# The first block's output projection in pairs of output tiles: seven half products in place of eight

## The reference, cut to what matters

```python
merged = g_ssm * (y_ssm @ w_proj_ssm) + g_att * (y_att @ w_proj_att)
x = x + gate * (merged @ w_out)        # w_out is 1024 x 1024
return rmsnorm(x, final_norm_w)        # goes into the second block
```

## Time and profile before

| | |
|---|---|
| median of 3 executions | 1833.75 us (1833.32 to 1833.89) |
| the profiled execution | 1833.91 us, its span 1832.4 us |
| PE busy | 1802.9 us (98%) |
| DVE, ACT, POOL busy | 1221.2 (67%), 744.7 (41%), 217.2 (12%) us |
| granted clock of TensorE, mean | 0.996 |
| stage 7, first matmul to first small product | 1111.45 to 1199.04 us |

### The profile page before, as it was taken

One profiled execution on the slowest core, in us unless ns is written; L12 is line 12 of the kernel. 1 busy time (PEld: TensorE's weight loads), 2 busy tenths in 40 slices (PEclk: granted clock), 3 DMA queues, 4 the chain that ended last, 5 costly groups with the idle time before them and its releaser, 6 DMA issues.

```text
span 1832.4 us, 26756 instructions
## 1 busy us (share of the span) xinstructions
PE 1802.9 (98%) x9827; PEld 1481.0 (81%) x9827; DVE 1221.2 (67%) x1630; ACT 744.7 (41%) x1145; POOL 217.2 (12%) x355
## 2 busy tenths in 40 slices
PE   7999999999999999999999999999999999999998
PEld 5788888888888888888888888878777778888886
DVE  4796455475377888888888444469366667676876
ACT  4423545553234454444445342353144445432422
POOL 2000011010102222012220000022100002110100
PEclk8999999999999999999999999999999999999999
DMA  9633765353611212122122843343311112210412
GB/s 298 236 62 64 153 120 104 99 155 120 184 58 47 81 58 61 42 80 80 58 57 103 296 145 99 117 131 95 112 35 49 37 34 58 58 47 22 146 33 104
DMA packets 176751, 180.45 MB, mean 98 GB/s; under 512 B 11171, under 2 KB 151896, under 8 KB 175768
## 3 DMA queue, kind: packets, MB, share of 16 engines
q1 hardware_dynamic: 162728, 129.95, 22.8%
q0 software_dynamic: 13920, 49.37, 11.5%
q10 hardware_dynamic: 16, 0.00, 0.0%
HBM read 138.80 MB, written 40.50 MB: 98 GB/s over the span
## 4 chain that ended last, share of the span: by engine, by line
PE 77%; PEld 12%; issue 3%; DVE 3%; ACT 2%; DMA 1%; DVEq 1%; SPq 0%; PEldq 0%; POOL 0%; POOLq 0%; ACTq 0%
PE acc L296 23%; PE acc L1713 16%; PE acc L315 14%; PEld acc L315 8%; PE acc L1741 3%; PE acc L3310 3%; PE work L1723 3%; PEld acc L296 2%; PE work L1733 2%; PE work L2743 1%; PE acc L621 1%; PE acc L2752 1%; PE work L2732 1%; PE acc L3648 1%; PEld acc L1115 1%
## 5 line engine op out<-in xcount | busy, mean ns | idle before, releaser
L315 PE MATMUL acc<-ha_hi,w_hi 128*128 128x512 f32 x640 | 257.4, 402 | 1.9 <-DVE nxt L2613 1.1
L315 PE MATMUL acc<-ha_hi,w_lo 128*128 128x512 f32 x640 | 249.9, 390 | 0.0
L315 PE MATMUL acc<-ha_lo,w_hi 128*128 128x512 f32 x640 | 249.3, 390 | 0.0
L276 DVE TENSOR_TENSOR w_lo<-w_raw,w_hi 128x1024 fp32r<-128x1024 f32 x94 | 115.4, 1228 | 92.8 <-ACT w_hi L272 90.5
L272 ACT ACTIVATE w_hi<-w_raw 128x1024 fp32r<-128x1024 f32 x92 | 97.0, 1055 | 188.7 <-PE acc L315 80.8
L296 PE MATMUL acc<-ha_hi,w_hi 128*128 128x512 f32 x528 | 164.9, 394 | 1.6 <-issue 1.0
L296 PE MATMUL acc<-ha_lo,w_hi 128*128 128x512 f32 x528 | 162.8, 389 | 0.0
L296 PE MATMUL acc<-ha_hi,w_lo 128*128 128x512 f32 x528 | 162.7, 389 | 0.0
L315 PEld LDWEIGHTS acc<-ha_hi,w_hi 128*128 128x128 f32 x640 | 120.2, 188 | 29.2 <-issue 5.0
L315 PEld LDWEIGHTS acc<-ha_hi,w_lo 128*128 128x128 f32 x640 | 120.1, 188 | 26.1
L315 PEld LDWEIGHTS acc<-ha_lo,w_hi 128*128 128x128 f32 x640 | 120.4, 188 | 22.6
(11 more groups left out here) (570 smaller groups left out, 3738.5 us busy)
## 6 DMA issues: line engine op xcount, KB each, us to landing
w_raw<-in_w_in SPq DMA_DIRECT2D x99, 512.0 KB, 4.0
ada_home<-in_w_ada SPq DMA_DIRECT2D x8, 1024.0 KB, 11.2
w_raw<-in_w_out SPq DMA_DIRECT2D x11, 512.0 KB, 4.0
x_tok<-in_x SPq DMA_DIRECT2D x8, 512.0 KB, 6.9
xt_scr<-xt SPq DMA_DIRECT2D x1, 4096.0 KB, 14.0
w_ada_g<-in_w_ada SPq DMA_DIRECT2D x8, 512.0 KB, 9.2
acs_even<-acs_scr POOLq DMA_DIRECT2D x4, 1024.0 KB, 15.9
acs_odd<-acs_scr POOLq DMA_DIRECT2D x4, 1024.0 KB, 15.9
```

Source lines behind the costliest of these rows:

```text
L276: dve.tensor_tensor(w_lo[:, n % 2, :, :], w_raw[:, n % 2, :, :], w_hi[:, n % 2, :, :].bitcast(F32), ALU.subtract).then_inc(lo_done, 1)
L315: mm = pe.matmul(acc[:, 0, half * HALF:(half + 1) * HALF], w[:, n % 2, k, :], x[:, k, half * HALF:(half + 1) * HALF], start=(k == 0 and i ...
```

## The change

Stage 7 takes its tiles two at a time, as a 2 x 2 product of 2 x 2 blocks: output rows 2p and 2p+1 by rows K1 and K2 of `merged` by tokens T1 and T2. In the seven-product form of Strassen and Winograd each pair is seven half products (M1 to M7) in place of eight: 28 in all for 32. With A the weights and X the activations in quarters:

- weights: S3 = A11 - A21, S2 = A22 - S3, S1 = A11 + S2, S4 = A12 - S2, each a DVE operation on 128x512, all but S2 in place in `w_raw`.
- activations: the differences T1' = X12 - X11 (here in words "the difference"), T3' = X22 - X12 (the "third sum", by POOL), T2' = X22 - T1' and T4' = X21 - T2', all in place in `merged`, whose memory also takes their low halves (`merged_r`).
- the order of the products is M1 (A11 X11), M5 (S1 T1'), M6 (S2 T2'), M2 (A12 X21), M7 (S3 T3'), M3 (S4 X22), M4 (A22 T4').
- the outputs: ACT keeps M1 and M5, each scaled by both gates; POOL adds what is kept to the row of x ahead of time (`pre_add`, six for each pair); DVE adds M6 and M7 to the common part (`add_common`) and evicts M6, M2, M3, M4.

Each product's weights are split on their own, in four half slots. `xt_tile` and the quarters of `w_out` come over SP's queue, the two loops of stage 6 are written out, and some of the new copies of the first pair stand at the end of stage 6, before the last merge. M6 of the first pair waits for all engines to have ended stage 6. The small products now wait for `acc_free` after DVE's last eviction. The diff, without the lines taken out (they stand above), and with eight columns of indent left out:

```diff
+M1, M5, M6, M2, M7, M3, M4 = range(7)
+def moving7(r, k):
+    return {M1: (ha_hi[:, k, T1], ha_lo[:, k, T1]), M5: (ha_hi[:, k, T2], ha_lo[:, k, T2]),
+            M6: (m2_hi[:, k, :], merged_r[:, k, T1]), M7: (m3_hi[:, k, :], merged_r[:, k, T2]),
+            M2: (ha_hi[:, KH + k, T1], ha_lo[:, KH + k, T1]), M3: (ha_hi[:, KH + k, T2], ha_lo[:, KH + k, T2]),
+            M4: (merged_r[:, KH + k, T2], merged_r[:, KH + k, T1])}[r]
+def bank7(p, r):
+    at = (2 + 7 * p + r) % 4
+    return accf[:, at * HALF:(at + 1) * HALF]
+def product_hi7(act, q):
+    p, r = divmod(q, 7)
+    if r in (M1, M4):
+        n = N_OUT1 + 2 * p + (r == M4)
+        act.wait_ge(w_loaded[n % 2], 16 * (n // 2 + 1))
+    elif r == M2 and p:
+        act.wait_ge(a12_loaded, A12_LOADED + 16 * p)
+    elif r in (M7, M6, M5, M3):
+        act.wait_ge(s_made, S_MADE + 4 * p + {M7: 1, M6: 2, M5: 3, M3: 4}[r])
+    act.wait_ge(mm_done, BASE7 + (-1 if q < 2 else q - 1 if q < 4 else 0 if q < 6 else q - 3))
+    act.activation(slot7(w_hi, q), weight7(r), ACT.Copy).then_inc(hi_done, 1)
+def product_lo7(dve, q):
+    dve.wait_ge(hi_done, BASE7 + q + 1)
+    dve.tensor_tensor(slot7(w_lo, q), weight7(q % 7), slot7(w_hi, q).bitcast(F32), ALU.subtract).then_inc(lo_done, 1)
+def sum_s3(dve, p):
...
+    dve.tensor_tensor(raw7("a21"), raw7("a11"), raw7("a21"), ALU.subtract)
+    dve.drain().then_inc(s_made, 1)
+def sum_s2(dve, p):
...
+    dve.tensor_tensor(w_sum7[:, :, :], raw7("a22"), raw7("a21"), ALU.subtract)
+    dve.drain().then_inc(s_made, 1)
+def sum_s1(dve):
+    dve.tensor_tensor(raw7("a11"), raw7("a11"), w_sum7[:, :, :], ALU.add)
+    dve.drain().then_inc(s_made, 1)
+def sum_s4(dve):
+    dve.tensor_tensor(raw7("a12"), raw7("a12"), w_sum7[:, :, :], ALU.subtract)
+    dve.drain().then_inc(s_made, 1)
...
+    project(pe, N_OUT1 - 1, ya_hi, ya_lo, row_read=rows_read6)
+    for j in range(KT):
+        if j + 1 < KT:
+            split_hi(act, N_MIX2 + j + 1)
+        sigmoid(j)
+        if j == KT - 1:
+            product_hi7(act, 0)
+            product_hi7(act, 1)
+            act.wait_ge(rows_read6, ROWS_READ6 + 2)
+            copy_hi(m2_hi[:, 0:3, :], merged[:, 0:3, T1])
+            act.wait_ge(t3_made, T3_MADE + 3)
+            act.wait_ge(rows_read6, ROWS_READ6 + 4)
+            act.activation(m3_hi[:, 0:3, :], merged[:, 0:3, T2], ACT.Copy).then_inc(m3_high, 1)
...
+    def merge(j):
+        projected(dve, n)
+        dve.tensor_tensor(gate6[:, b, :], acc[:, n % 2, :], gate6[:, b, :], ALU.mult).then_inc(acc_free[n % 2], 1)
+        dve.drain()
+        dve.wait_ge(mix_loaded[b], 16 * (j // 2) + 16)
+        dve.tensor_tensor(merged[:, j, :], gate6[:, b, :], mix_before[:, b, :], ALU.add)
+        dve.drain().then_inc(gate6_used, 1)
+    for j in range(KT - 1):
+        split_lo(dve, N_MIX2 + j + 1)
+        merge(j)
...
+        else:
+            dve.tensor_tensor(merged[:, i, T1], merged[:, j, T2], merged[:, i, T1], ALU.subtract)
+            copy_lo(2 * j, ha_lo[:, j, :], merged[:, j, :], ha_hi[:, j, :])
+            dve.drain()
+            dve.tensor_tensor(merged[:, j, T1], merged[:, j, T1], merged[:, i, T1], ALU.subtract)
+            dve.drain().then_inc(t_made, 1)
+            if j == KT - 2:
+                sum_s3(dve, 0)
+                sum_s2(dve, 0)
+            copy_lo(2 * j + 1, merged_r[:, j, T1], merged[:, j, T1], merged_r[:, j, T2])
+    product_lo7(dve, 0)
+    dve.drain()
+    sum_s1(dve)
+    product_lo7(dve, 1)
+    copy_lo(2 * KT - 2, merged_r[:, 0:3, T1], merged[:, 0:3, T1], m2_hi[:, 0:3, :])
+    n, b, j = N_OUT1 - 1, (KT - 1) % 2, KT - 1
+    dve.wait_ge(gate6_done, KT)
+    projected(dve, n)
+    dve.wait_ge(mix_loaded[b], 16 * (j // 2) + 16)
+    for half in (T2, T1):
+        last = dve.tensor_tensor(gate6[:, b, half], acc[:, n % 2, half], gate6[:, b, half], ALU.mult)
+        dve.drain()
+        dve.tensor_tensor(merged[:, j, half], gate6[:, b, half], mix_before[:, b, half], ALU.add)
+        dve.drain()
+        if half == T2:
+            dve.tensor_tensor(merged[:, KH - 1, T1], merged[:, j, T2], merged[:, KH - 1, T1], ALU.subtract)
+            dve.drain().then_inc(t_made, 1)
+    dve.drain().then_inc(acc_free[n % 2], 1)
+    dve.drain().then_inc(gate6_used, 1)
...
+    def third_sum(i):
+        pool.wait_ge(gate6_used, KH + i + 3)
+        pool.tensor_tensor(merged[:, i, T2], merged[:, KH + i, T2], merged[:, i, T2], ALU.subtract)
+        pool.drain().then_inc(t3_made, 1)
+    for j in range(KT):
+        if j >= KH + 2:
+            third_sum(j - KH - 2)
+    third_sum(2)
+    pool.wait_ge(m3_high, M3_HIGH + 1)
+    pool.tensor_tensor(merged_r[:, 0:3, T2], merged[:, 0:3, T2], m3_hi[:, 0:3, :].bitcast(F32), ALU.subtract
+                       ).then_inc(m3_low, 1)
+    third_sum(3)
...
+    def load_part(p, tile, half, done, signal):
+        sp.wait_ge(lo_done, BASE7 + 7 * (p - 1) + done + 1)
+        sp.dma_start(w_raw[:, (O0, O1)[tile], (K1, K2)[half], :],
+                     cols(io["w_out"], (2 * p + tile) * P)[:, (K1, K2)[half], :]).then_inc(signal, 16)
+    for p in range(OUT_PAIRS):
+        if p + 1 < OUT_PAIRS:
+            load_part(p + 1, 0, 0, M5, w_loaded[O0])
+        if p == 0:
+            sp.wait_ge(gate6_used, KT + 2)
+        for i in range(2):
+            load_xt(2 * p + i)
+        if p + 1 < OUT_PAIRS:
+            load_part(p + 1, 1, 0, M7, a21_loaded)
+            load_part(p + 1, 0, 1, M3, a12_loaded)
+            load_part(p + 1, 1, 1, M4, w_loaded[O1])
...
+    pe.wait_ge(acc_free[O0], N_OUT1 // 2)
+    for p in range(OUT_PAIRS):
+        for r in range(7):
+            q = 7 * p + r
+            pe.wait_ge(lo_done, BASE7 + q + 1)
+            if q == M6:
+                begin_stage(pe, 7)
+            if r <= M2 and p:
+                pe.wait_ge(evicted7, EVICTED7 + 5 * (p - 1) + r + 2)
+            if r in (M7, M3):
+                pe.wait_ge(kept7, KEPT7 + 2 * p + 1 + (r == M3))
+            if r == M4:
+                pe.wait_ge(evicted7, EVICTED7 + 5 * p + 1)
+            w_h, w_l = slot7(w_hi, q), slot7(w_lo, q)
+            for k in range(KH):
+                if p == 0 and r in (M1, M5):
+                    pe.wait_ge(x_lo_done, LO6 + 2 * k + 1 + (r == M5))
+                if q == M6:
+                    pe.wait_ge(x_lo_done, LO6 + (2 * KT - 1 if k < KH - 1 else LOW_T2 + 1))
+                if q == M2 and k == KH - 1:
+                    pe.wait_ge(x_lo_done, LO6 + LOW_X2 + 1)
+                if q == M7 and k in (0, KH - 1):
+                    pe.wait_ge(m3_low, M3_LOW + (1 if k == 0 else 2))
+                if q == M4 and k == KH - 1:
+                    pe.wait_ge(x_lo_done, LO6 + ROW_T4 + 1)
+                hi, lo = moving7(r, k)
+                for i, (w, x) in enumerate(((w_h, hi), (w_l, hi), (w_h, lo))):
+                    mm = pe.matmul(bank7(p, r), w[:, k, :], x, start=(k == 0 and i == 0),
+                                   stop=(k == KH - 1 and i == 2))
...
+    def keep_first(p):
+        product_done(7 * p + M1)
+        if p:
+            act.wait_ge(pre_added, PRE_ADDED + 6 * p)
+        act.activation(kept1_0[:, :], bank7(p, M1), ACT.Copy, scale=gate7(p, 0))
+        act.activation(common[:, :], bank7(p, M1), ACT.Copy, scale=gate7(p, 1)).then_inc(kept7, 1)
+    def keep_second(p):
+        product_done(7 * p + M5)
+        act.activation(kept5_0[:, :], bank7(p, M5), ACT.Copy, scale=gate7(p, 0))
+        act.activation(kept5_1[:, :], bank7(p, M5), ACT.Copy, scale=gate7(p, 1)).then_inc(kept7, 1)
...
+    act.wait_ge(t_made, T_MADE + KT)
+    act.activation(m2_hi[:, KH - 1, :], merged[:, KH - 1, T1], ACT.Copy).then_inc(x_hi_done, 1)
+    product_hi7(act, 2)
+    act.wait_ge(gate6_used, KT + 2)
...
+    keep_first(0)
+    act.wait_ge(t3_made, T3_MADE + KH)
+    act.activation(m3_hi[:, KH - 1, :], merged[:, KH - 1, T2], ACT.Copy).then_inc(m3_high, 1)
+    product_hi7(act, 3)
+    keep_second(0)
+    act.wait_ge(t_made, T_MADE + KT + 1)
+    act.activation(merged_r[:, KT - 1, T2], merged[:, KT - 1, T1], ACT.Copy).then_inc(x_hi_done, 1)
+    for q in range(4, 7):
+        product_hi7(act, q)
...
+    def add_common(p, r):
+        dve.wait_ge(mm_done, BASE7 + 7 * p + r + 1)
+        dve.wait_ge(kept7, KEPT7 + 2 * p + 1)
+        dve.scalar_tensor_tensor(common[:, :], bank7(p, r), gate7(p, 1), common[:, :], ALU.mult, ALU.add)
+        return dve.drain()
+    def evict(p, r, row_of, half, pre, out=True):
+        dve.wait_ge(mm_done, BASE7 + 7 * p + r + 1)
+        dve.wait_ge(pre_added, PRE_ADDED + 6 * p + pre)
+        x = xt_tile[:, row_of, half]
+        dve.scalar_tensor_tensor(res[:, 2 * p + row_of, half] if out else x, bank7(p, r), gate7(p, row_of), x,
+                                 ALU.mult, ALU.add).then_inc(evicted7, 1)
...
+    product_lo7(dve, 2)
+    copy_lo(ROW_X2, ha_lo[:, KT - 1, :], merged[:, KT - 1, :], ha_hi[:, KT - 1, :])
+    dve.drain()
+    dve.wait_ge(t3_made, T3_MADE + KH)
```

(79 more changed lines are left out.)

257 lines of the change are left out of this document (145 added, 112 removed).

## The result

| | before | after |
|---|---|---|
| median (lowest to highest) | 1833.82 us (1833.32 to 1834.86) | 1852.30 us (1851.48 to 1853.98) |
| ratio, 95% interval | | 1.0096 (1.0085 to 1.0108) |
| profiled execution: time, span | 1833.9, 1832.4 us | 1853.98, 1852.3 us |
| mean granted clock | 0.996 | 0.990 |

The change costs 18.5 us, in a stage from which 10.9 us of matmuls were taken. The forecast was +10.5.

The account below looks back on a forecast made before the run. PE was taken to bound stage 7, busy 87.05 of 87.10 us. Terms -10.9 + 10.7 + 2.4 + 8.3 = +10.5 us on the profiled 1833.9 gave 1844 us; range 1829 to 1856.

Parts of the forecast that it names:

- The sign: Whole kernel: slower, +10.5 us; chances 0.65 slower, 0.16 same, 0.19 faster.
- the forecast's own case: Whole kernel: the summed terms give 1844 us, own range 1838 to 1851; chance 0.50.
- rival 2: Entry: PE's clock falls after a pause of 5.7 us, about +5, 1849 us; chance 0.15.
- Rival 1: Whole stage: POOL's short operations don't hold DVE, sum -3.7, 1830 us; chance 0.19 of this case, faster.
- A: Stage 7's matmuls: 28 half products stay of 32, 48 matmuls at 0.227 us removed, -10.9 us.
- B: Entry, M1 to M7 of the first pair: DVE and POOL work delays M6 and M7, +10.7 us.
- C: Pairs, after M7 of the first: DVE held by POOL doesn't catch up, +2.4 us (0 to +6).
- with POOL's 6 x 1.1 = 6.6: Pairs: six POOL additions at 1.1 us each, held against DVE's 16.6 us, make 23.2 us for each pair.
- D: Exit: small products wait for DVE's last eviction, 8.8 us in place of 0.5, +8.3 us.
- Costed at nothing: Pairs: ACT's work, the eight `xt_tile` loads moved to SP's queue and four part loads for each pair, 0 us.
- POOL's third sums as work of 1.1 us: Entry: each third sum priced as one POOL operation of 1.1 us.
- end of the last mix projection at 1111.0: Entry: the walk's times counted from 1111.0, the last mix projection's end.

Follow-up runs that it names:

- e5: Changed kernel with 20 of POOL's 24 additions ahead of the evictions left out of the computation: 1843.29 us, ratio 1.0042.
- e10: Changed kernel with 6 of DVE's 7 sums of squares in the stage left out of the computation: 1846.05 us, ratio 1.0070.
- e1: Changed kernel with useless matmuls put into PE's three longest pauses of the stage: 1850.97 us, ratio 1.0098.
- e7: Changed kernel with the entry reordered (last merge first, M7's low halves on DVE, third sums signalled without a drain): 1850.92 us, ratio 1.0082.
- e2: Changed kernel with the small products' banks handed over once last M7 is read, their weights multiplied first, going row by row: 1849.43 us, ratio 1.0086.
- e3: Changed kernel with xt rows loaded straight into res, so no load waits for the pair before's evictions: 1852.81 us, ratio 1.0103.
- e4: Changed kernel with POOL's third sums signalled by the addition itself in place of a drain behind it: 1850.77 us, ratio 1.0092.

## Why the prediction was right, and where it was short

**The sign, and why.** Right, in the mechanism named: PE stops being the bound, DVE becomes it, and POOL holds it. e5 and e10 show it directly. The size was short: 1852.3 us lies within the whole range (1829 to 1856), but above the forecast's own case (1838 to 1851) and above rival 2's 1849. Rival 1 (POOL holding nothing) fell with the 3.23 us of the last merge and S1's 1.58.

**A** came as computed. **B**: M6 11.1 us after M1, walked through as 11.15; M7 20.6 for 21.5. This sum was right, with POOL's price too low (3.69 us where I had 3.0, 1.27 to 1.30 where I had 1.1). The slow clock in M6 and M2, which it didn't hold, was hidden behind DVE: with a full clock (e1) M7's low weights come 20.8 us after M1. e7 adds what the walk couldn't show: the entry's delay is DVE's backlog, and most of what is cut in the entry alone comes back in the pairs.

**C** was the mis-sized term: +5.1 for +2.4. The step was "with POOL's 6 x 1.1 = 6.6": they take 1.87 each, since DVE holds POOL as well as POOL DVE (1.44 in e10, with DVE's sums left out). I had halved durations of 1024 elements from places where POOL had one operation of DVE beside it, not a stream of them, and took 1.4 for a bound that was none.

**D**: +8.7 for +8.3, as walked through: the wait was for the last eviction, DVE's work up to it took 11.0 us for 11.2, and DVE came to it late. What I didn't see is that this wait is of the program's making: the small products needed only a bank that had been read 8 us earlier (e2). In rival 1 I had taken D at 4, where the bound that I gave for it was 3; it changes nothing here.

**Costed at nothing.** The `xt_tile` loads: right (e3). POOL's third sums as work of 1.1 us: wrong, the drain behind them waits for row loads, signals 3.5 us later and moves M1 by 1.7 (e4). The step that failed here is "end of the last mix projection at 1111.0", taken as given.

**Rival 2, the clock.** I gave it as the other case, at +5, in the entry. It did fall there, to 0.57, and once more at M7, to 0.66, but this costs 0.3 us by e2 and 0.2 by e1; the cost is in the exit, 2.6 us in the small products, after a pause that the forecast itself had put at 8.8 us. It should have been a term of the sum. The Trainium skill (TensorE: Matmul & The Clock Gate, HAM oscillation — how this bites in real kernels) says that pauses bring the lower clock: this trace agrees, with 0.57 after 5.4 us and 0.50 after 8.8, but whether it costs time hung on who was the bound.

So of the 8.2 us between +10.5 and +18.7, by where they lie, 2.7 are C, 1.7 the drain and 4.2 the clock; B came 1.0 cheaper, D and what follows 0.7 dearer. By cause the clock is 2.9 of them and C 4.0, since in e2 DVE's waits took most of the 1.6 us of M7 and M3 when the clock was full. The range held since its upper end had POOL at 1.4 and part of the clock; that the 1.87 and the cost in the exit stayed under it is partly luck.

## What to carry to other kernels

When matmuls are traded for sums on other engines, add up what those engines do in the same stretch, with each POOL operation counted twice, for POOL and for DVE; if that comes near PE's new time, the saving is gone, and moving the work about in time only moves the wait. A wait that the chain names need not be worth anything (the load here), and one that fits a count of work may be a semaphore given too late (the bank). Where the forecast itself has PE pause for many microseconds, price the slower clock on the far side of the pause, but only where PE is then the bound.

## What the runs showed of the hardware

- DVE and POOL hold each other: additions on 128x512 on POOL took 1.87 us in the pairs, 1.44 there with six of DVE's sums left out (e10), and the four third sums 1.27 to 1.30. DVE's took 1.58 in place of 0.69, and 3.23 beside a POOL operation of 3.69. Reading PSUM, DVE took 0.69 and 0.75 beside the same operations.
- POOL's drain behind two row loads that it had just issued signalled 3.5 us after the addition before it had ended, 0.1 to 0.6 us after the second load had landed; with no load just before, the drain ended 0.1 us after the addition. Signalling from the addition itself took this away.
- After 5.4 us without matmuls PE went on at a clock of 0.57, after 8.8 us at 0.50 (the small products took 6.27 us for 3.64). Around M7 it fell to 0.66 in after, behind a pause of 1.9 us, and stayed at 1.00 in e2, behind one of 1.6. With matmuls of no use in the pauses it stayed at 1.00.
